# Taking the best sums of the gathered tile early, and giving a quarter of its row products to POOL and ACT

## The reference, cut to what matters

```python
def peer_ffn(x, wq, sub1, sub2, u_tab, v_tab):        # x: 512 tokens x 1024, after RMSNorm
    q = (x @ wq).reshape(B, S, 8, 256)                # 8 heads
    s1 = q[..., :128] . sub1                          # 128 scores per head
    s2 = q[..., 128:] . sub2                          # 128 scores per head
    v1, i1 = top_k(s1, 16); v2, i2 = top_k(s2, 16)
    cand = v1[..., :, None] + v2[..., None, :]        # 256 sums per head
    top_s, pos = top_k(cand, 16)                      # best 16 sums
    idx = take(i1 * 128 + i2, pos)                    # 128 experts per token
    wgt = softmax(top_s)
    act = gelu(u_tab[idx] . x)
    return sum(wgt * act * v_tab[idx])                # per token
```

## Time and profile before

| | |
|---|---|
| median of 3 runs | 4760.27 us (4757.66 to 4764.66) |
| profiled execution | 4777.11 us, span 4775.3 us |
| mean granted clock of PE | 0.972 |
| busy in the span | PE 4448.6, PEld 3691.8, DVE 3138.8, POOL 2693.7, ACT 1810.5 us |
| DMA | 891.87 MB, mean 187 GB/s |
| first layer's query rounds | about 1010 to 1112 us |
| first layer's chunk stage | about 1114 to 1841 us |

### The profile page before, as it was taken

The page is one execution under the profiler, slowest core; times in us unless marked ns, Lnnn a source line. Parts: engine busy times, 40 slices in busy tenths (PEclk is TensorE's granted clock), DMA queues, the critical chain, the costliest instruction groups (busy, mean ns, idle before and its releaser), DMA issues.

```text
span 4775.3 us, 73532 instructions
## 1 busy us (share of the span) xinstructions
PE 4448.6 (93%) x21322; PEld 3691.8 (77%) x21322; DVE 3138.8 (66%) x5007; ACT 1810.5 (38%) x3307; POOL 2693.7 (56%) x1477
## 2 busy tenths in 40 slices
PE   7999999999999998999989999999999898889998
PEld 5766775789889897777767667757898898877776
DVE  5754223448889776888867541244488897668888
ACT  2234114124566652333332341231245666533333
POOL 5743663665456675555558436636654566655554
PEclk9999999999999999999999999999999999999999
DMA  3211221224689999999822112212246899999997
GB/s 105 80 49 36 80 81 47 70 78 137 182 259 283 298 318 329 335 343 333 292 87 84 49 36 83 79 42 75 80 142 192 260 288 302 335 315 343 340 338 268
DMA packets 467060, 891.87 MB, mean 187 GB/s; under 512 B 45600, under 2 KB 324640, under 8 KB 463776
## 3 DMA queue, kind: packets, MB, share of 16 engines
q1 hardware_dynamic: 387424, 617.22, 40.1%
q0 software_dynamic: 73728, 268.47, 16.2%
q10 hardware_dynamic: 5696, 3.85, 0.3%
HBM read 786.61 MB, written 102.76 MB: 186 GB/s over the span
## 4 chain that ended last, share of the span: by engine, by line
PE 61%; DVE 12%; issue 11%; DMA 8%; POOL 3%; ACT 3%; SPq 1%; DVEq 0%; ACTq 0%; POOLq 0%; another core or an unknown queue 0%
PE pair L824 6%; DMA ring<-v_tab 5%; PE bank L1230 5%; PE bank L824 5%; PE bank L1235 5%; PE bank L1225 4%; PE bank L1173 4%; PE bank L850 3%; PE pair L850 3%; PE pair L826 3%; PE bank L826 3%; PE bank L990 2%; PE bank L1177 2%; DMA ring<-u_tab 2%; DVE qk L2329 1%
## 5 line engine op out<-in xcount | busy, mean ns | idle before, releaser
L678 POOL TENSOR_TENSOR w_hi<-ring,ones 128x1024 fp32r<-128x1024 f32 x272 | 536.4, 1972 | 844.8 <-PE bank L850 277.8
L666 POOL TENSOR_TENSOR w_lo<-ring,w_hi 128x1024 fp32r<-128x1024 f32 x256 | 615.8, 2406 | 539.8 <-ACT w_hi L1628 532.3
L1173 PE MATMUL bank<-xT,w_hi 128*128 128x384 f32 x2048 | 720.3, 352 | 40.0 <-ACT gst L1640 36.4
L681 POOL TENSOR_TENSOR w_lo<-ring,w_hi 128x1024 fp32r<-128x1024 f32 x272 | 693.8, 2551 | 21.3
L1173 PE MATMUL bank<-xl_peer,w_hi 128*128 128x384 f32 x2048 | 698.8, 341 | 0.0
L1634 ACT CAST w_hi<-ring 128x1024 fp32r<-128x1024 f32 x252 | 266.0, 1056 | 671.7 <-PE bank L1235 445.3
L1628 ACT CAST w_hi<-ring 128x1024 fp32r<-128x1024 f32 x256 | 269.6, 1053 | 598.6 <-DVE ring L2297 427.8
L2389 DVE TENSOR_TENSOR cl<-att,ch 128x384 fp32r<-128x384 f32 x256 | 354.8, 1386 | 172.6 <-ACT ch L1699 165.6
L672 POOL TENSOR_TENSOR w_lo<-ring,w_hi 128x1024 fp32r<-128x1024 f32 x126 | 301.8, 2395 | 280.5 <-ACT w_hi L1634 280.5
L1173 PEld LDWEIGHTS bank<-xT,w_hi 128*128 128x128 f32 x2048 | 397.3, 194 | 43.1 <-ACT w_hi L1628 34.6
L1225 PE MATMUL bank<-w_hi,ch 128*128 128x512 f32 x1524 | 392.1, 393 | 21.4 <-ACT ch L1699 21.4
(11 more groups left out here) (360 smaller groups left out, 9332.8 us busy)
## 6 DMA issues: line engine op xcount, KB each, us to landing
ring<-v_tab SPq DMA_DIRECT2D x252, 512.0 KB
ring<-w_stream SPq DMA_DIRECT2D x240, 512.0 KB
ring<-u_tab SPq DMA_DIRECT2D x512, 128.0 KB
g_spill<-gst SPq DMA_DIRECT2D x256, 192.0 KB
hn<-u_tab SPq DMA_DIRECT2D x256, 128.0 KB
x_last<-u_tab SPq DMA_DIRECT2D x256, 128.0 KB
w_spill<-vg SPq DMA_DIRECT2D x12, 2048.0 KB
w_spill<-att SPq DMA_DIRECT2D x12, 2048.0 KB
```

The source lines that it names most:

```text
L666: nc.gpsimd.tensor_tensor(w_lo[s % 2][:, :], ring[2 + s % 2][:, :], w_hi[s % 2][:, :].bitcast(F32), ALU.subtract)\
L678: nc.gpsimd.tensor_tensor(w_hi[b][:, 0:n], src, ones[:, 0:1].to_broadcast([P, n]), ALU.mult)\
L681: nc.gpsimd.tensor_tensor(w_lo[b][:, 0:n], src, w_hi[b][:, 0:n].bitcast(F32), ALU.subtract)\
L1173: nc.tensor.matmul(out, w_hi[s % 2][:, c * P:(c + 1) * P], dense_parts(c)[part], start=(c == 0 and part == 0), stop=False)
```

## The change

- **Best sums in the query rounds.** After each of the first three query rounds' `best_keys`, DVE makes the 256 sums of that round's two heads of the gathered tile and takes the best 16 of them (`sparse_heads`). The loop over these rounds is written out. The fourth round's heads follow in the chunk stage.
- **Half decoded first.** The gathered tile's choice (`sparse_choice`) begins with decoding its first four heads into table indices, at chunks 2 to 6 (9 pieces). The dense tile 0's choice moves to chunks 7 to 23. The rest of the gathered choice (20 pieces) lies in chunks 24 to 31, and tile 1's begins at chunk 32 instead of 34.
- **Rows earlier.** The first six gathers stand at chunk 8, and rows are used from chunk 11 on: 8 in chunks 11 to 23, 112 over the 96 one-hot chunks, 8 over the last 8.
- **Shared rows.** Rows 0 to 7 and every fourth row after them (`SHARED_ROWS`, 38 of 128) are not dotted by DVE: POOL multiplies the row with the token vectors (`row_times`, behind the low part of its chunk), and ACT sums it (`row_sum`, ahead of the gelu). DVE copies the token vectors from PSUM to `nwb` once for this. The gather that reuses a shared row's buffer waits for ACT's sum.
- ACT's loops over chunk rounds become written-out code, its exponential for tile 0 (`soft(0, wts)`) moves one round later.

```diff
-ROWS = [0] * (4 * LEAD + 14) + shares(18, 18) + shares(40, 32) + shares(54, 32) + shares(16, 8) \
+ROWS = [0] * 11 + shares(8, 4 * LEAD - 11) + shares(112, 4 * WROUNDS) + shares(8, 8) \
     + [0] * 4 + shares(SLOTS, NCHUNK - 4)
+FIRST_ROW = [sum(ROWS[:c]) for c in range(NCHUNK + 1)]
+SHARED_ROWS = [n for n in range(SLOTS) if n < FIRST_ROW[4 * LEAD] or n % 4 == 3]
...
             def gather(L, table, n):
-                if n >= NG:
-                    pool.wait_ge(g_used.sem, g_used.at(L, "U", 0, n - NG + 1))
+                m = n - NG
+                if m >= SLOTS:
+                    pool.wait_ge(g_used.sem, g_used.at(L, "V", 0, m - SLOTS + 1))
+                elif m in SHARED_ROWS:
+                    pool.wait_ge(row_summed.sem, row_summed.at(L, "U", 0, shared_at(m)))
+                elif m >= 0:
+                    pool.wait_ge(g_used.sem, g_used.at(L, "U", 0, m + 1 - shared_at(m)))
+                if n == HS:
+                    pool.wait_ge(eidx_ready.sem, eidx_ready.at(L, "T", 0, 2))
...
+            def row_times(L, n):
+                if n == SHARED_ROWS[0]:
+                    pool.wait_ge(row_ready.sem, row_ready.at(L, "N2", 0, 1))
+                pool.wait_ge(g_ready[n % NG], landed(L, n))
+                stand(pool)
+                nc.gpsimd.tensor_tensor(grow[n % NG], grow[n % NG], nwb[:, :], ALU.mult).then_inc(row_product.sem, 1)
...
                     if c < NCHUNK:
                         expert_low(L, c // 4, c % 4)
+                        for m in shared_rows(c):
+                            row_times(L, m)
...
-                    if c == 4 * LEAD + 11:
-                        pool.wait_ge(eidx_ready.sem, eidx_ready.at(L, "T", 0, 2))
+                    if c == 8:
+                        pool.wait_ge(eidx_ready.sem, eidx_ready.at(L, "T", 0, 1))
...
+                def row_sum(n):
+                    act.wait_ge(row_product.sem, row_product.at(L, "U", 0, shared_at(n)))
+                    nc.scalar.activation(grow[n % NG], grow[n % NG], ACT.Copy, accum_out=actv[:, n:n + 1])\
+                        .then_inc(row_summed.sem, 1)
...
+                        for n in shared_rows(4 * i + s) if isinstance(i, int) else ():
+                            row_sum(n)
                         gelu_of(i, s)
...
+                def sparse_heads(c, best, where):
+                    v = kval.rearrange("p (h a t) n -> p t h a n", a=2, t=TT)[:, SP_T, :, :, :]
+                    both = cand[:, 0:2, :]
+                    c.step(V.tensor_tensor(both.rearrange("p h (a b) -> p h a b", a=TOPK),
+                                           v[:, :, 0, :].unsqueeze(3).to_broadcast(pair_of),
+                                           v[:, :, 1, :].unsqueeze(2).to_broadcast(pair_of), ALU.add))
+                    for n in range(2):
+                        for j in range(2):
+                            c.step(V.max(best(j)[n], both[:, j, :]))
...
+                        for j in range(2):
+                            c.step(V.max_index(where(j)[n], best(j)[n], both[:, j, :]))
...
+                        if n == 0:
+                            for j in range(2):
+                                c.step(V.match_replace(both[:, j, :], best(j)[n], both[:, j, :], NEG * 1e8))
...
+                for i in range(LAST):
+                    with dve.Fori(0, 1):
+                        keys_wait(i)
+                        for _ in best_keys(c, i, 0, TT):
+                            pass
+                        dve.sem_inc(best_done.sem, 1)
...
+                        for _ in sparse_heads(c, lambda j: slice_of(tv_s, i, j), lambda j: slice_of(posu_s, i, j)):
+                            pass
...
+                def sparse_choice():
+                    c.step(V.tensor_copy(idx_p[:, 0:HH, :, :], idxf[:, SP_T, :, :].rearrange("p (h a) n -> p h a n", a=2)[:, 0:HH, :, :]))
+                    yield
+                    yield from experts_of(0)
+                    yield from best_keys(last_keys, LAST, SP_T, SP_T + 1)
+                    copy_indices(c, SP_T)
+                    yield from sparse_heads(c, lambda j: slice_of(tv_s, LAST, j), lambda j: slice_of(posu_s, LAST, j))
+                    yield from experts_of(1)
...
+                V.tensor_copy(nwb[:, :], pair[:, :]).then_inc(row_ready.sem, 1)
...
-                early = 12
-                pieces = [shares(upto, 4 * LEAD - 8) + [0, 1], [0] * (4 * LEAD - 6) + shares(early, 4)]
+                sooner, later = 1 + 8, 5 + 6 + 8 + 1
+                pieces = [[0] * 5 + shares(upto, 16) + [1], shares(sooner, 5)]
...
-                used = 0
-                pieces = [shares(upto - early, 10), [0] * 10 + shares(upto, 20) + [0, 1], [0] * 32 + shares(upto, 30) + [0, 1]]
+                used = FIRST_ROW[4 * LEAD]
+                pieces = [shares(later, 8), [0] * 8 + shares(upto, 22) + [0, 1], [0] * 32 + shares(upto, 30) + [0, 1]]
...
                     for _ in range(ROWS[n]):
-                        dot(used)
+                        if used not in SHARED_ROWS:
+                            dot(used)
                         used += 1
```

More of the change, by code:

```diff
@@ L477, in build, with landed, shared_rows, shared_at @@
         TURN_BANK = dict(N1=[4, 5, 6, 7, 0, 1, 2, 3], N2=list(range(8)))
+        def landed(L, n):
+            return 16 * (L * -(-(2 * SLOTS - n % NG) // NG) + n // NG + 1)
+        def shared_rows(c):
+            return [n for n in range(FIRST_ROW[c], FIRST_ROW[c + 1]) if n in SHARED_ROWS]
+        def shared_at(n):
+            return len([m for m in SHARED_ROWS if m <= n])
         def drnd(L, phase, i):
@@ L746, in _ @@
                 split_rounds(L, "WQ")
-                with pool.Fori(0, LEAD + 2) as r:
+                with pool.Fori(0, 2) as r:
                     for c in range(4):
@@ L1678, in _ @@
                     expert_high(0, s)
-                with act.Fori(0, LEAD - 2) as i:
+                with act.Fori(0, 2) as i:
                     round_of(i)
+                stand(act)
+                with act.Fori(0, 1):
+                    for i in range(2, LEAD - 1):
+                        round_of(i)
                 soft(0, wts)
-                round_of(LEAD - 2)
                 round_of(LEAD - 1, tile=0)
@@ L1690, in _ @@
                         round_of(LEAD + 8 * d + y, k=8 * d + y, tile=DENSE if y < 7 else d + 1)
-                with act.Fori(LEAD + WROUNDS, ROUNDS["UE"] - 1) as i:
-                    round_of(i)
+                stand(act)
+                with act.Fori(0, 1):
+                    for i in range(LEAD + WROUNDS, ROUNDS["UE"] - 1):
+                        round_of(i)
                 round_of(ROUNDS["UE"] - 1, last=True)
@@ L2185, in keys_wait, with slice_of @@
                     stand(dve)
[L2187 to L2193, removed]
-                    stand(dve)
+                def slice_of(buf, i, j):
+                    at = 2 * TOPK * i + TOPK * j
+                    return [buf[:, at + 8 * n:at + 8 * n + 8] for n in range(2)]
@@ L2198, in _, with decode @@
                 small = [P, PEER_H, TOPK]
+                def decode(c, part, pos, first, second):
+                    hs = slice(HH * part, HH * part + HH)
+                    ks = slice(HS * part, HS * part + HS)
+                    c.step(V.tensor_scalar(posu2[:, 0, :], pos[:, ks], 4, None, ALU.logical_shift_right))
+                    c.step(V.tensor_scalar(posu2[:, 1, :], pos[:, ks], 15, None, ALU.bitwise_and))
+                    c.wait()
+                    c.step(V.tensor_copy(pos_p[:, 0, :], posu2[:, 0, :]))
+                    c.step(V.tensor_copy(pos_p[:, 1, :], posu2[:, 1, :]))
+                    c.wait()
+                    yield
+                    for half, e in enumerate((first, second)):
+                        eq3 = eqb.rearrange("p (k n) -> p k n", n=TOPK)
+                        c.step(V.tensor_tensor(eq3, pos_p[:, half, :].unsqueeze(2).to_broadcast([P, HS, TOPK]),
+                                               iota_f[:, :].unsqueeze(1).to_broadcast([P, HS, TOPK]), ALU.is_equal))
+                        c.wait()
+                        yield
+                        eq4 = eqb.rearrange("p (h k n) -> p h k n", h=HH, n=TOPK)
+                        c.step(V.tensor_tensor(eq4, eq4, idx_p[:, hs, half, :].unsqueeze(2).to_broadcast(full), ALU.mult))
+                        c.wait()
+                        yield
+                        c.step(V.tensor_reduce(e, eq3, AX.X, ALU.add))
+                        c.wait()
+                        yield
@@ L2200, in choose @@
                 def choose(t, w):
[L2202 to L2203 removed]
+                    c = Chain(dve, choose_step, L, "T", t)
                     v4 = vals[:, t, :, :].rearrange("p (h a) n -> p h a n", a=2)
[L2205 to L2208 removed]
@@ L2221, in choose @@
                     for part in range(2):
-                        hs = slice(HH * part, HH * part + HH)
                         ks = slice(HS * part, HS * part + HS)
@@ L2404, in _ @@
```

(2 more changed lines are left out.)

127 lines of the change are left out of this document (73 added, 54 removed).

## The result

| | before | after |
|---|---|---|
| median of 4 runs | 4760.23 us (4757.66 to 4764.66) | 4815.77 us (4809.95 to 4827.41) |
| profiled execution | 4777.11, span 4775.3 | 4811.21, span 4809.4 |
| ratio | | 1.0118 [1.0097, 1.014] |

The kernel got 55 us slower, where 34 us of gain were forecast. The time lies outside the predicted range and on the other side.

A forecast was written before the change was run, and what follows sets the result against it. The prediction took DVE to bound A to C and late table chunks to delay D and E. Its terms summed to -17 us per layer, -34 in both, from 4760.27 to 4726; range 4680 to 4775.

The forecast's parts named there:

- C: Chunks 56 to 87, 188 us: DVE bounds, 41 dots become 28; -14 us per layer (-10 to -20).
- B: Chunks 32 to 55, 143 us: as many dots, about 4 us of sparse choice gone; -3 us (0 to -5).
- rival (2): Gain eaten: loop from one-hot to ACT's scaling to PE holds C, bursts keep D and E; 4760; chance 0.17.
- Coupling: Chunks 24 to 127: 30 shared rows load POOL and ACT, PE may wait; +3 us per layer (0 to +8).
- rival (3): One-hot chunks: POOL's queue becomes bound, low parts behind gathers waiting for ACT's sum; +26 per layer, 4812 us; chance 0.13.
- Query rounds: Before chunk 0: DVE's added best sums of two heads delay PE's start; +8 us per layer (+4 to +13).
- Lead: Chunks 0 to 23: POOL's gathers and products make PE wait for low parts; +7 us per layer (+2 to +12).
- A: Chunks 24 to 31, 46 us: 20 later choice pieces and 7 dots load DVE; +6 us (5 to 9).
- D: Chunks 88 to 119, 183 us: fewer rows fetched, waits for the table mostly go; -16 us (-12 to -20).
- E: Chunks 120 to 127, 54 us: eight rows fewer, the long table wait shortens; -8 us (-4 to -12).

## Why the prediction was wrong, step by step

**C and B: the step that failed.** It is "DVE is the bound there", with -14 for C and -3 for B out of DVE's load. Measured: -2.3 and +3.1 for C, +10.4 and +6.1 for B. DVE at 87% and ACT waiting for its transpose were read as a full engine. They are as well what a loop through DVE looks like. With the dots on DVE, C is shorter with more DVE work; and with the one-hots last and the same work C is 14 and 12 us shorter in the two layers of the changed kernel. This decides for the loop. In it stood PE's one-hot product, DVE's one-hots, pieces, dots and transpose, ACT's high part, sum, gelu, copy and scaling. The prediction had this as rival (2), at 0.17, but left C at -7 and thought of no price for the new sum in it.

**Coupling: mis-sized.** +3 per layer was taken, with ACT's sums counted as room on an engine that has some. They cost 0.46 us of time each with the dots left on DVE, 17 per layer; POOL's product cost 6 per layer and the gather's wait for the sum 11. The last is 0.3 us per shared row, so the wait of rival (3) alone did not reach its point of decision of 0.5 us; ACT's sum added 0.46. That rival (3) names 4812 and 4816 was measured is luck: it had 46 us per layer for sharing, measured are 25, and -20 for all the rest, measured are +3.

**Query rounds: right in mechanism.** +8 was taken, +9.5 and +10.5 measured. Ahead of the next round's keys DVE now waits 1.01 us where it had 4.78, as in the first row here. The sum of two SBUF inputs took 0.69 us after the first round and the third, and 2.47 after the second, where it began beside a low part of POOL's, the third row:

```profile
1064.81 3.19 DVE L2214 MAX8 big<-big 128x8 f32<-128x128 f32 x16 [1.01 <-DVE att L2263]
...
1086.55 2.47 DVE L2250 TENSOR_TENSOR att<-big 128x512 f32<-128x512 f32 x1 [0.33 <-DVE big L2229]
```

```profile
1085.94 2.52 POOL L717 TENSOR_TENSOR w_lo<-ring,w_hi 128x1024 fp32r<-128x1024 f32 x1
```

So the hold by POOL exists, in one of the three rounds of each layer. The Trainium skill, "SBUF — State Buffer", section "Who interferes with whom", has a DVE instruction with two SBUF inputs locked out while GpSimd reads SBUF; the trace agrees with up to 1.8 us in one of these sums.

PE's wait ahead of chunk 0 grew from 1.70 to 11.68 us, where about 8 were expected:

```profile
1124.41 0.68 PE L1211 MATMUL bank<-xT,w_hi 128*128 128x384 f32 x1 [11.68 <-ACT w_hi L1666]
```

**Lead: right in part, too small.** +7 was taken, +11.8 and +11.6 measured, at the upper bound of 12. The waits from 1112 to 1232 show PE behind POOL's low parts, as forecast, after the wait ahead of chunk 0:

```profile
PE bank L1211 <- ACT w_hi L1666: 11.7, 1, 11.7
...
PEld bank L1215 <- POOL w_lo L702: 7.0, 5, 2.7
...
PE bank L1215 <- POOL w_lo L702: 5.3, 3, 2.4
```

This is about half of the growth. The one-hots' place took 3.5 and 2.9 us off the lead (113.4 and 113.8), so part of it comes from DVE's order at the first one-hot chunks. And with the dots on DVE and no product on POOL the lead is 113.9 and 116.8 all the same, though PE then waits for a low part only once, 2.4 us. What makes up the remainder stays open.

**A: the number right, by luck in part.** +6 was taken, +7.6 and +7.0 measured. DVE's load rose by 4 us only (46.6 for 42.3), and with the one-hots last the same kernel takes 45.2 and 45.6 in A, about the 45.4 of the kernel before. So here too the order counted, and not the load alone.

**D: right in mechanism.** -16 was taken, -12.5 and -11.7 measured, at the small end. Seventeen rows fewer do relieve the table's transfers: the DMA share fell from 1.03 to 0.99 and the rate from 315 to 286 GB/s, and PE is busy for 97% of it. The moved dots play no part, since D is 168.0 with all dots on DVE. DVE's waits for the table, 18.7 us before, are halved, where the prediction had them mostly gone:

```profile
DVE ring L2421 <- DMA ring<-u_tab: 9.7, 5, 6.2
```

**E: too large.** -8 was taken, -3 measured. The one long wait for the table was to shorten; it grew from 12.2 us to 19.8:

```profile
DVE ring L2421 <- DMA ring<-u_tab: 19.8, 1, 19.8
```

What of it the stores and what the value stage's first loads make wasn't tried.

Per layer the miss is 39 to 41 us: B and C together give 25 or 26 of it, E and the lead 5 each, D 4, query and A 3 to 4; the coupling's +3 comes off, since it is measured inside the stretches.

## What to carry to other kernels

Where every engine has idle time and the stretch still doesn't shrink, follow one item round the engines until you are back at the first one: everything that stands between two of its steps in an in-order queue is on the path, also on the engine that is busy the least. Ask of each piece of work in a queue whether it stands between an input that has just come and an output that somebody waits for; moving the pieces and dots, which nobody in the loop waited for, ahead of the 1.3 us one-hots was worth 24 us to the kernel before and 77 to the changed one, with no instruction less. And before work is shared out to an engine with idle time, put the bare instruction there without its data and time it: that told 35 us for 94 us of work on ACT, and 13 for 182 on POOL. Such a price belongs to the order it was measured in: once the one-hots came last, sharing cost nothing that was measured in the changed kernel's layout.

## What the runs showed of the hardware

PE's granted clock was halved after a wait. Ahead of chunk 0 the changed kernel's PE stood still for 11.7 us; then its granted clock was 0.50, that is 1.2 of 2.4 GHz, in the 3.6 us of this window and in the 1.1 us behind it:

```profile
1124.40:1128.00 3.60, 3.59 (x11) 3.60 (x12) 3.48 (x4) 1.05 (x1) 3.60 (x2) 0.50 0.53 146
```

Products of 384 columns started 0.32 us apart there, and 0.17 us apart later. The kernel before, whose PE waited 1.70 us at this place, ran through the lead at a granted 1.00. PE's first 24 products took 6.5 us instead of 4.4. The kernel's time hardly shows these 2 us: the gelu of chunk 0 starts 9.0 us after PE's first product in both kernels, and the kernel before with the heads in the query rounds, whose PE waited 11.67 us and then had a granted 0.51, has a lead of 105.2 (before 105.1).

POOL held DVE in a regular way. Of the eight sums of two SBUF inputs in the changed kernel (line 2250, 128x512), four began while POOL made a low part; they took 2.46 to 2.69 us, and each ended 0.55 us after POOL's instruction. The other four took 0.69. A copy on DVE with one SBUF input and an SBUF output, 128x256, was held as well. It took 0.29 us between the query rounds before, and 1.12 and 1.09 in the changed kernel, once in each layer, where it began beside a product of POOL's and ended 0.15 us after it:

```profile
1084.90 1.12 DVE L2229 COPY big<-big 128x256 f32<-128x256 f32 x1
```

```profile
1083.97 1.89 POOL L714 TENSOR_TENSOR w_hi<-ring,ones 128x1024 fp32r<-128x1024 f32 x1 [1.07 <-PE pair L864]
```
